# The last chunk of each norm added, squared and summed in two token halves, with fewer identity products around its sums

## The chip, the cores and the metric

The kernel runs on one core of a Trainium2 chip. A core has TensorE (PE, matrix products into PSUM banks; its weight loader is listed apart as PEld), VectorE (DVE), ScalarE (ACT), GpSimd (POOL) and a queue for DMAs (SyncE, SP). They run side by side and wait for one another by semaphores. The metric is the time of one execution on the device in microseconds, lower is better.

## The reference

Two transformer-like blocks on x of 512 tokens by 1024 channels, float32. The first has one layer, modulated by a conditioning vector; the second has two layers. Between their parts stand RMS norms:

```python
def _rmsnorm_2(x, g):
    x32 = x.astype(jnp.float32)
    y = x32 * lax.rsqrt(jnp.mean(x32 * x32, axis=-1, keepdims=True) + RMS_EPS)
    return (y * g.astype(jnp.float32)).astype(x.dtype)

def second_block(x, norm_g, ffn_w_gate, ffn_w_up, ffn_w_down, w_in, conv_w, pool_w, pool_scale, w_out):
    for l in range(DEPTH_2):
        g = norm_g[l]
        f = _swiglu(_rmsnorm_2(x, g[0]), ffn_w_gate[l, 0], ffn_w_up[l, 0], ffn_w_down[l, 0])
        x = x + 0.5 * _rmsnorm_2(f, g[1])
        m = _mixer(_rmsnorm_2(x, g[2]), w_in[l], conv_w[l], pool_w[l], pool_scale[l], w_out[l])
        x = x + _rmsnorm_2(m, g[3])
        f = _swiglu(_rmsnorm_2(x, g[4]), ffn_w_gate[l, 1], ffn_w_up[l, 1], ffn_w_down[l, 1])
        x = x + 0.5 * _rmsnorm_2(f, g[5])
    return x
```

The first block is a mixer (attention and a state-space branch) and a feed-forward part, each behind a modulated norm and added to x through a gate (`gt1`, `gt2`), and a final norm. What matters here is the sum of squares over the 1024 channels, for each token: it needs every channel before any token can be scaled.

## The kernel before

Everything lies with channels on the 128 partitions: x is 8 chunks of 128 channels by 512 tokens (`x[:, c, :]`, `DC` = 8, `T` = 512). A linear layer is a row of *units*; one unit makes one chunk of 128 output channels in one PSUM bank (`unit_bank[s]`, s = 0 or 1 in turn; two units are a *pair* p). Weights and inputs are split into a high and a low part, and each unit multiplies high by high, high by low and low by high (L649 to L651). While TensorE multiplies, SyncE loads later weights, ACT and POOL split them (L1211, L510), and DVE takes finished banks.

Each engine's program is written out by hand in one order; nothing is scheduled later. Waits are `e.wait_ge(semaphore, count)`.

A norm sits between the last unit of one layer and the first of the next. Its work on the eight chunks c = 0 to 7 goes along with the last eight units: DVE takes the bank (`take`, L2211, L2216 or L2220), ACT squares the chunk (`f_squares`: L1228 into `f_sq`, and L1230 into `gf_sq`, scaled by a gain, for the norm that follows), DVE adds the squares to a running sum and, in norms 1 to 5, the products of x and f too (`cross_of`, L2155, and L2158). After chunk 6 the sum of seven chunks is `f_acc`.

The last chunk is what this case is about. TensorE turns squares into sums for each token with `token_sums` (L704): four products with a column of ones, one for each block of 128 tokens, into four columns of a bank. It does so first for `f_acc`, then for the square of the last chunk, `f_sq`, and the two are added up in PSUM. Then ACT takes the root (L1221), DVE the reciprocal (L2193), and `spread` on TensorE (L712) copies the factor of each token to all partitions. DVE updates x chunk by chunk (L2233, L2235), ACT and POOL split the new input, and TensorE starts on it in `first_units` (L725, L735). Between these steps stands `keep_warm(n)` (L699): n products of the identity matrix with itself, whose result nobody reads. A product of float32 values stands in the trace as two records, in the order as one row.

`norm(r)` does this for r = 0 (end of the first block) to 5. The last norm, r = 6, works by token halves already: `last_unit` on TensorE, `last_halves` on DVE (L2104, L2114), and its squares on ACT (L1260). `halves` are the columns 0 to 255 and 256 to 511.

The norm in the middle of the first block (the x1 norm here) is written out apart: DVE's `take_update` (L2021) adds the gated output to x, ACT squares it (`square`, L1217, called from `squares_along`), TensorE sums `x_acc` and then the last square, turns a row of modulation values (`turn_ada`, L925) that ACT has copied (`take_row`, L1326) and spreads the inverse (L1154). ACT takes the root in L1470, DVE the inverse in L2040, and then the gate values (L1791, L1785).

Of the kernel before, what the change touches and what calls it, by code (L numbers as in the profile page):

```python
# [104 lines left out]
def program(nc, d):  # L105
    ctx = ExitStack()
    with ctx:
# [3 lines left out]
        def sem(name):  # L111
            return ctx.enter_context(nc.semaphore(name))
# [190 lines left out]
        pool_step, turn_ready = sem("pool_step"), sem("turn_ready")  # L303
        vec_passed = sem("vec_passed")
        out_stored = sem("out_stored")
        f_scaled, x_summed = sem("f_scaled"), sem("x_summed")

        def col(name, i=0, n=1):
# [326 lines left out]
        def _(e):  # L635
# [60 lines left out]
            def keep_warm(n, bank=mix[1]):  # L696

                for _ in range(n):
                    e.matmul(bank[:, 0:P], tab("ident"), tab("ident"), start=True, stop=True)  # L699

            def token_sums(sums, src, first=True, last=True):

                for b in range(TB):
                    mm = e.matmul(sums[:, b:b + 1], src[:, b * P:(b + 1) * P], tab("ones", 0, 1),  # L704
                                  start=first and b == 0, stop=last and b == TB - 1)
                return mm

            def spread(n, inv, bank):
# [94 lines left out]
            def norm(r):  # L803


                e.wait_ge(fsq_added, (DC - 1) * (r + 1))
                token_sums(square_sum, f_acc, last=False)
                keep_warm(3)
                e.wait_ge(fsq_ready, 2 * DC * r + 2 * (DC - 1) + 1)
                token_sums(square_sum, f_sq, first=False).then_inc(sums_ready, 1)  # L810
                keep_warm(3)
                spread(2 * r + 1, inv_f, stat_bank)

                e.wait_ge(cross_ready, r + 1)
                mm = token_sums(gf_sum, gf_acc)
                if r:
                    mm = token_sums(cross_sum, cross_acc)
                mm.then_inc(cross_sums, 1)
                keep_warm(4)
                first_units(FIRST_OF_NORM + r, 6, lambda: spread(2 * r + 2, inv_u, mix[1]))  # L820
# [322 lines left out]
            sum_rows(score[0])  # L1143
            e.wait_ge(sq_used, DC - 1)
            token_sums(square_sum, x_acc, last=False)
            keep_warm(3)
            e.wait_ge(sq_ready, DC)
            token_sums(square_sum, sq[:, 1, :], first=False).then_inc(x1_sums, 1)
            keep_warm(1)
            turn_ada(2, score[1], TB)  # L1150
            keep_warm(2)
            e.wait_ge(x1_inverse, 1)
            for b in range(TB):
                mm = e.matmul(stat_bank[:, b * P:(b + 1) * P], inv_f[:, b:b + 1].broadcast_to([P, P]), tab("ident"),  # L1154
# [44 lines left out]
        def _(e):  # L1199
# [13 lines left out]
            def square(q, c):  # L1213

                if c >= 2:
                    e.wait_ge(sq_used, DC * q + c - 1)
                e.activation(sq[:, c % 2, :], x[:, c, :], ACT.Square).then_inc(sq_ready, 1)  # L1217
# [5 lines left out]
            def f_squares(p, s, part, c, g):  # L1223

                e.wait_ge(taken[s], p + 2)
                settled()
                fc = part[:, bass.ds(c, 1), :].rearrange("p a t -> p (a t)")
                e.activation(f_sq, fc, ACT.Square).then_inc(fsq_ready, 1)  # L1228
                if g is not None:
                    e.activation(gf_sq, fc, ACT.Square, scale=g(c)).then_inc(fsq_ready, 1)  # L1230

            def first_high(q, s):

                e.wait_ge(first_loaded[s], 16 * (q + 1))
                e.activation(first_hi[:, s, :], first_raw[:, s, :], ACT.Copy).then_inc(first_hi_ready, 1)

            def norm(r, p, part, g):
# [19 lines left out]
                if not ahead:  # L1257
# [16 lines left out]
                            store(n - 1)  # L1274
                    store(len(PE_SUMS) - 1)
                    return
                f_squares(p, 1, part, DC - 1, g)
                e.wait_ge(sums_ready, r + 1)
                token_root(root_f, square_sum)
                for c in range(DC):  # L1280
# [169 lines left out]
            def squares_along(q, p0, refills):  # L1450

                for c in range(DC):
                    if c:
                        e.wait_ge(taken[(c - 1) % 2], p0 + (c - 1) // 2 + 2)
                        square(q, c - 1)
                    if c == refills - 1:
                        for s in range(2):
                            first_high(0, s)
                    if c < refills:
                        refill(p0 + c // 2 + 1, c % 2)  # L1460
                e.wait_ge(taken[1], p0 + DC // 2 + 1)
                square(q, DC - 1)
                take_row(2 * DC + 1, 2, score[0][:])

            e.preload_act_table_set("sqrt_and_others")
# [166 lines left out]
        def _(e):  # L1632
# [10 lines left out]
            def flat(ap):  # L1643
                return ap.rearrange("p a t -> p (a t)")
# [372 lines left out]
            def take_update(p, s, c, gate):  # L2017
# [3 lines left out]
                e.scalar_tensor_tensor(xc, unit_bank[s][:], mod[:, bass.ds(gate + c, 1)], xc, ALU.mult,  # L2021
                                       ALU.add).then_inc(taken[s], 1)

            step(e.memset(stat_bank[:], 0.0))
            for k in range(DC):
                add_ada(k, 64, 2 * DC, ada_shift[k % 3], (*score, *mix), shift_sum)
                if k:
                    e.wait_ge(sq_ready, k)
                    step(e.tensor_tensor(x_acc if k == DC - 1 else stat_bank[:], stat_bank[:], sq[:, (k - 1) % 2, :],
                                         ALU.add))  # L2030
                    e.sem_inc(sq_used, 1)
                take_update(OUT1 + k // 2, k % 2, k, 16)
            def gated_update(p0, gate):
                with e.Fori(0, DC // 2) as i:
                    for s in range(2):
# [98 lines left out]
            def norm(r, p, take, part, g, update):  # L2134
# [25 lines left out]
                def chunk(p, s, c, ahead_of_last=0):  # L2160


                    e.wait_ge(unit_done, 2 * p + s + 1)
                    direct = crossed and take is take_new and ahead_of_last != 1
                    if direct:
                        cross_of(c, unit_bank[s][:])
                    take(p, s, c)
                    if crossed and not direct:
                        e.wait_ge(taken[s], p + 2)
                        cross_of(c, row(f, c))  # L2170
                    if crossed:
                        add_cross(cross_acc if ahead_of_last == 1 else cross_run)
                    if ahead_of_last == 1:
                        return
                    e.wait_ge(fsq_ready, 2 * DC * r + (2 if ahead else 1) * c + 1)
                    step(e.tensor_tensor(f_acc if ahead_of_last == 2 else f_run, f_run, f_sq, ALU.add))
                    if ahead:
                        add_gf(c, gf_run)
                    e.sem_inc(fsq_added, 1)
# [26 lines left out]
                                           ALU.mult, ALU.subtract).then_inc(u_last, 1)  # L2206
                e.wait_ge(rstd_ready, r + 1)

            def take_x(p, s, c):
                xc = flat(x[:, bass.ds(c, 1), :])  # L2210
                e.scalar_tensor_tensor(xc, unit_bank[s][:], mod[:, bass.ds(40 + c, 1)], xc, ALU.mult,  # L2211
                                       ALU.add).then_inc(taken[s], 1)

            def take_f(p, s, c):
                fc = flat(f[:, bass.ds(c, 1), :])
                e.tensor_tensor(fc, unit_bank[s][:], fc, ALU.add).then_inc(taken[s], 1)  # L2216

            def take_new(p, s, c):
                settled()
                e.tensor_copy(flat(f[:, bass.ds(c, 1), :]), unit_bank[s][:]).then_inc(taken[s], 1)  # L2220

            def final_norm(c):
                e.scalar_tensor_tensor(x[:, c, :], x[:, c, :], col("g_final", c), stat_bank[:], ALU.mult,
# [307 lines left out]
```

## Time and profile before

| | us |
|---|---|
| median of 3 runs | 2482.87 |
| lowest, highest | 2482.63, 2484.28 |
| the profiled execution | 2483.62 |
| its span (first to last instruction) | 2481.8 |
| TensorE busy in it | 2468.1 |
| DVE, ACT, POOL busy | 1172.6, 917.1, 1078.8 |

The span is what the trace covers; 1.8 us of the profiled execution lie around it. TensorE's busy time counts the identity products too, so a busy TensorE isn't always a useful one. All times below are microseconds from the start of the span, unless marked ns. The norms' sums of the last chunk stand at 334, 605, 971, 1170, 1537, 1905 and 2103 us of the span.

### The profile page before, as it was taken

To read this page: it belongs to the slowest core of one execution; us is meant where nothing else is said; L and a number is where in the kernel's file an instruction comes from. 1 tells how busy PE (TensorE), PEld (TensorE's weight loads), DVE (VectorE), ACT (ScalarE), POOL (GpSimd) and SP (SyncE) were. 2 spreads that over 40 slices of the span, in tenths; PEclk is the share of its full clock that TensorE was granted. 3 is DMA by queue.
4 is the path that set the end of the run, shared out by engine and by line. 5 is a ranking of instruction groups with operands and counts; after the bars stand their busy time and mean duration, and the time that the engine had idled before them with its cause. 6 is when DMAs were issued, how large, how long until landed. Compare 5 with 4: busy or idle time off the path is not lost.

```text
span 2481.8 us, 33166 instructions
## 1 busy us (share of the span) xinstructions
PE 2468.1 (99%) x11577; PEld 2012.0 (81%) x11577; DVE 1172.6 (47%) x1726; ACT 917.1 (37%) x1307; POOL 1078.8 (43%) x535
## 2 busy tenths in 40 slices
PE   9999999999999999999999999999999999999999
PEld 6777888888888888778888888888888778888887
DVE  7574866264331345676431345331345676431332
ACT  4444443235321334554331234321234454431332
POOL 5333454445344445334444445444445334444444
PEclk9999999999999999999999999999999999999999
DMA  6222643322223221322233232233231322232232
GB/s 253 86 81 92 232 171 118 110 93 77 92 101 105 100 101 62 101 77 93 76 104 107 95 105 72 85 106 106 93 109 61 93 79 100 76 103 86 99 106 81
DMA packets 74059, 253.43 MB, mean 102 GB/s; under 512 B 9184, under 2 KB 13408, under 8 KB 73856
## 3 DMA queue, kind: packets, MB, share of 16 engines
q1 hardware_dynamic: 73408, 251.93, 29.8%
q8 instruction: 44, 0.72, 0.1%
q10 hardware_dynamic: 576, 0.52, 0.1%
q14 instruction: 31, 0.25, 0.0%
HBM read 244.76 MB, written 2.10 MB: 99 GB/s over the span
## 4 chain that ended last, share of the span: by engine, by line
PE 86%; issue 9%; POOL 3%; DVE 2%; ACT 0%; DMA 0%; SPq 0%; POOLq 0%; DVEq 0%; ACTq 0%
PE unit_bank L649 26%; PE unit_bank L650 26%; PE unit_bank L651 26%; POOL w_lo L510 2%; PE score L735 2%; PE score L725 1%; PE mix L868 1%; PE out_bank L848 1%; PE mix L699 1%; PE mix L876 0%; PE out_bank L704 0%; PE score L868 0%; POOL u_lo L609 0%; PE stat_bank L712 0%; DVE arena L1662 0%
## 5 line engine op out<-in xcount | busy, mean ns | idle before, releaser
L510 POOL TENSOR_TENSOR w_lo<-raw,w_hi 128x1024 fp32r<-128x1024 f32 (+2 forms) x374 | 954.2, 2551 | 1301.7 <-ACT w_hi L1211 1301.5
L1211 ACT ACTIVATE w_hi<-raw 128x1024 fp32r<-128x1024 f32 (+2 forms) x375 | 416.1, 1110 | 1203.2 <-PE unit_bank L651 1181.9
L649 PE MATMUL unit_bank<-u_hi,w_hi 128*128 128x512 f32 x2152 | 843.0, 392 | 1.2 <-POOL w_lo L510 1.2
L650 PE MATMUL unit_bank<-u_lo,w_hi 128*128 128x512 f32 x2152 | 837.8, 389 | 0.0
L651 PE MATMUL unit_bank<-u_hi,w_lo 128*128 128x512 f32 x2152 | 837.7, 389 | 0.0
L649 PEld LDWEIGHTS unit_bank<-u_hi,w_hi 128*128 128x128 f32 x2152 | 403.9, 188 | 101.3 <-issue 14.3
L651 PEld LDWEIGHTS unit_bank<-u_hi,w_lo 128*128 128x128 f32 x2152 | 404.0, 188 | 84.6
L650 PEld LDWEIGHTS unit_bank<-u_lo,w_hi 128*128 128x128 f32 x2152 | 404.0, 188 | 82.5 <-issue 0.2
L649 PE MATMUL unit_bank<-h_hi,w_hi 128*128 128x512 f32 x981 | 382.7, 390 | 0.2 <-DVE h_lo L2080 0.2
L651 PE MATMUL unit_bank<-h_hi,w_lo 128*128 128x512 f32 x981 | 381.7, 389 | 0.0
L650 PE MATMUL unit_bank<-h_lo,w_hi 128*128 128x512 f32 x981 | 381.6, 389 | 0.0
L2263 DVE TENSOR_TENSOR arena<-unit_bank,rstd 128x512 f32<-128x512 f32 x84 | 58.1, 691 | 398.9 <-PE unit_bank L651 398.9
L649 PEld LDWEIGHTS unit_bank<-h_hi,w_hi 128*128 128x128 f32 x981 | 184.2, 188 | 39.2 <-DVE h_lo L2080 0.7
L650 PEld LDWEIGHTS unit_bank<-h_lo,w_hi 128*128 128x128 f32 x981 | 184.2, 188 | 38.5 <-issue 0.5
L651 PEld LDWEIGHTS unit_bank<-h_hi,w_lo 128*128 128x128 f32 x981 | 184.1, 188 | 38.4
L2272 DVE TENSOR_TENSOR h_lo<-arena,h_hi 128x512 f32 (+1 forms) x88 | 170.9, 1942 | 78.5 <-ACT h_hi L1535 78.5
L2220 DVE COPY f<-unit_bank 128x512 f32 (+1 forms) x48 | 33.2, 691 | 204.2 <-PE unit_bank L651 202.7
L2260 DVE TENSOR_TENSOR arena<-unit_bank,rstd 128x512 f32<-128x512 f32 x84 | 58.1, 691 | 119.4 <-PE unit_bank L651 119.4
L1535 ACT ACTIVATE h_hi<-arena 128x512 f32 (+1 forms) x88 | 55.6, 632 | 34.0 <-DVE arena L2270 33.4
L2216 DVE TENSOR_TENSOR f<-unit_bank,f 128x512 f32 (+1 forms) x31 | 21.4, 690 | 91.8 <-PE unit_bank L651 90.8
L2270 DVE TENSOR_TENSOR arena<-arena 128x512 f32<-128x512 f32 x88 | 60.9, 693 | 3.3
L609 POOL TENSOR_TENSOR u_lo<-arena,u_hi 128x512 fp32r<-128x512 f32 x42 | 53.2, 1301 | 8.4 <-ACT arena L1477 8.2
(383 smaller groups left out, 2074.4 us busy)
## 6 DMA issues: line engine op xcount, KB each, us to landing
raw<-in_w_gate_up SPq DMA_DIRECT2D x168, 512.0 KB, 3.4
raw<-in_w_down SPq DMA_DIRECT2D x64, 704.0 KB, 4.1
raw<-in_w_in SPq DMA_DIRECT2D x65, 512.0 KB, 3.5
raw<-in_w_up SPq DMA_DIRECT2D x30, 512.0 KB, 3.5
f<-in_w_ada_rows SPq DMA_DIRECT2D x26, 512.0 KB, 5.4
raw<-in_w_out SPq DMA_DIRECT2D x24, 512.0 KB, 3.5
raw<-in_w_down SPq DMA_DIRECT2D x16, 512.0 KB, 3.5
ada_in_u<-in_w_ada SPq DMA_DIRECT2D x8, 512.0 KB, 11.1
```

Source lines behind the costliest of these rows:

```text
L510: e.tensor_tensor(w_lo[:, s, 0:n], raw[:, s, 0:n], as32(w_hi[:, s, 0:n]), ALU.subtract).then_inc(lo_ready, 1)
L609: e.tensor_tensor(u_lo[:, c, :], u_all[:, c, :], as32(u_hi[:, c, :]), ALU.subtract).then_inc(u_ready, 1)
L649: e.matmul(bank[:], wh, hi(k), start=n == 0, stop=False)
L650: e.matmul(bank[:], wh, lo(k), start=False, stop=False)
L651: mm = e.matmul(bank[:], wl, hi(k), start=False, stop=last)
L735: e.matmul(score[s][:], w[:, s, c * P:(c + 1) * P], u_hi[:, c, :], start=c == 0 and w is first_hi, stop=False)
L1211: e.activation(w_hi[:, s, 0:n], raw[:, s, 0:n], ACT.Copy).then_inc(hi_ready, 1)
L1535: e.activation(h_hi[:, bass.ds(i, 1), :].rearrange("p a t -> p (a t)"), ffn_h, ACT.Copy).then_inc(hhi_ready, 1)
L2260: g = e.tensor_tensor(ffn_g, banks[0][:], rstd[:], ALU.mult)
L2263: u = e.tensor_tensor(ffn_u, banks[1][:], rstd[:], ALU.mult)
L2270: e.tensor_tensor(ffn_h, ffn_s, ffn_u, ALU.mult).then_inc(hidden_ready, 1)
L2272: e.tensor_tensor(flat(h_lo[:, bass.ds(i, 1), :]), ffn_h, as32(flat(h_hi[:, bass.ds(i, 1), :])), ALU.subtract).then_inc(h_ready, 1)
```

## The change

The addition of chunk 7 on DVE becomes two operations of 256 tokens each, in the six norms and in the x1 norm. ACT squares each half as soon as it is there, on semaphores of their own (`last_taken` and `taken[1]`, `x_half_taken` and `taken[1]`), and the scaled square into `gf_sq` follows in one piece. TensorE sums blocks 0 and 1 when the first half is squared, blocks 2 and 3 when the second is (`sums_by_halves`). The identity products before and after these sums go from three and three to one and one in the six norms; in the x1 norm those before the sums (three), between the sums and the turn (one) and behind the turn (two) go.

```diff
-            def token_sums(sums, src, first=True, last=True):
-
-                for b in range(TB):
+            def token_sums(sums, src, first=True, last=True, blocks=range(TB)):
+
+                for b in blocks:
                     mm = e.matmul(sums[:, b:b + 1], src[:, b * P:(b + 1) * P], tab("ones", 0, 1),
                                   start=first and b == 0, stop=last and b == TB - 1)
+                return mm
+
+            def sums_by_halves(src, squared, at):
+
+                for hf in range(2):
+                    e.wait_ge(squared, at + hf + 1)
+                    mm = token_sums(square_sum, src, first=False, blocks=(2 * hf, 2 * hf + 1))
                 return mm
...
                 token_sums(square_sum, f_acc, last=False)
-                keep_warm(3)
-                e.wait_ge(fsq_ready, 2 * DC * r + 2 * (DC - 1) + 1)
-                token_sums(square_sum, f_sq, first=False).then_inc(sums_ready, 1)
-                keep_warm(3)
+                keep_warm(1)
+                sums_by_halves(f_sq, last_squared, 2 * r).then_inc(sums_ready, 1)
+                keep_warm(1)
                 spread(2 * r + 1, inv_f, stat_bank)
...
             token_sums(square_sum, x_acc, last=False)
-            keep_warm(3)
-            e.wait_ge(sq_ready, DC)
-            token_sums(square_sum, sq[:, 1, :], first=False).then_inc(x1_sums, 1)
-            keep_warm(1)
+            sums_by_halves(sq[:, 1, :], x_half_squared, 0).then_inc(x1_sums, 1)
             turn_ada(2, score[1], TB)
-            keep_warm(2)
             e.wait_ge(x1_inverse, 1)
...
+            def last_squares(r, p, part, g):
+
+                e.wait_ge(last_taken, r + 1)
+                settled()
+                for hf, cs in enumerate(halves):
+                    if hf:
+                        e.wait_ge(taken[1], p + 2)
+                    e.activation(f_sq[:, cs], part[:, DC - 1, cs], ACT.Square).then_inc(last_squared, 1)
+                e.activation(gf_sq, part[:, DC - 1, :], ACT.Square, scale=g(DC - 1)).then_inc(fsq_ready, 2)
...
-                f_squares(p, 1, part, DC - 1, g)
+                last_squares(r, p, part, g)
...
-                e.wait_ge(taken[1], p0 + DC // 2 + 1)
-                square(q, DC - 1)
+                e.wait_ge(sq_used, DC * q + DC - 2)
+                for hf, cs in enumerate(halves):
+                    if hf:
+                        e.wait_ge(taken[1], p0 + DC // 2 + 1)
+                    else:
+                        e.wait_ge(x_half_taken, 1)
+                    e.activation(sq[:, (DC - 1) % 2, cs], x[:, DC - 1, cs], ACT.Square).then_inc(x_half_squared, 1)
...
+            def last_update(p, gate):
+
+                c = DC - 1
+                e.wait_ge(unit_done, 2 * p + 2)
+                for cs, done in zip(halves, (x_half_taken, taken[1])):
+                    e.scalar_tensor_tensor(x[:, c, cs], unit_bank[1][:, cs], mod[:, gate + c:gate + c + 1], x[:, c, cs],
+                                           ALU.mult, ALU.add).then_inc(done, 1)
...
-                    take(p, s, c)
+                    if ahead_of_last == 1:
+                        for cs, done in zip(halves, (last_taken, taken[s])):
+                            take(p, s, c, cs, done)
+                    else:
+                        take(p, s, c)
...
-            def take_f(p, s, c):
-                fc = flat(f[:, bass.ds(c, 1), :])
-                e.tensor_tensor(fc, unit_bank[s][:], fc, ALU.add).then_inc(taken[s], 1)
+            def take_f(p, s, c, cs=slice(0, T), done=None):
+                fc = flat(f[:, bass.ds(c, 1), cs])
+                e.tensor_tensor(fc, unit_bank[s][:, cs], fc, ALU.add).then_inc(done or taken[s], 1)
```

`take_x` and `take_new` get the same two arguments. `ahead_of_last == 1` marks the last chunk.

TensorE in norm 1, from the sums of `f_acc` (first row) to the spread of the inverse. `arena` holds the squares and their sums, `tabs` the identity and the ones, `mix1` is the bank that the identity products write. Before:

```order
L704 MATMUL out_bank<-tabs,arena 128x1 [waits fsq_added]
L704 MATMUL out_bank<-tabs,arena 128x1 x3
L699 MATMUL mix1<-tabs 128x128 x3
L704 MATMUL out_bank<-tabs,arena 128x1 [waits fsq_ready]
L704 MATMUL out_bank<-tabs,arena 128x1 x3
L699 MATMUL mix1<-tabs 128x128 x3
L712 MATMUL stat_bank<-tabs,arena 128x128 [waits inverse_ready]
```

The same stretch of TensorE in the changed kernel:

```order
L706 MATMUL out_bank<-tabs,arena 128x1 [waits fsq_added]
L706 MATMUL out_bank<-tabs,arena 128x1 x3
L701 MATMUL mix1<-tabs 128x128
L706 MATMUL out_bank<-tabs,arena 128x1 [waits last_squared]
L706 MATMUL out_bank<-tabs,arena 128x1
L706 MATMUL out_bank<-tabs,arena 128x1 [waits last_squared]
L706 MATMUL out_bank<-tabs,arena 128x1
L701 MATMUL mix1<-tabs 128x128
L721 MATMUL stat_bank<-tabs,arena 128x128 [waits inverse_ready]
```

The wait for the square has become two, one for each half, and four of six identity products are gone.

TensorE in the x1 norm, from the sums of `x_acc` to the spread (L1154, later L1158), with the turn of the modulation row (L925, later L933) between. Before:

```order
L704 MATMUL out_bank<-tabs,arena 128x1 [waits sq_used]
L704 MATMUL out_bank<-tabs,arena 128x1 x3
L699 MATMUL mix1<-tabs 128x128 x3
L704 MATMUL out_bank<-tabs,arena 128x1 [waits sq_ready]
L704 MATMUL out_bank<-tabs,arena 128x1 x3
L699 MATMUL mix1<-tabs 128x128
L925 MATMUL score1<-tabs,arena 128x128 [waits row_ready]
L925 MATMUL score1<-tabs,arena 128x128 x3
L699 MATMUL mix1<-tabs 128x128 x2
L1154 MATMUL stat_bank<-tabs,arena 128x128 [waits x1_inverse]
```

The same stretch of TensorE in the changed kernel:

```order
L706 MATMUL out_bank<-tabs,arena 128x1 [waits sq_used]
L706 MATMUL out_bank<-tabs,arena 128x1 x3
L706 MATMUL out_bank<-tabs,arena 128x1 [waits x_half_squared]
L706 MATMUL out_bank<-tabs,arena 128x1
L706 MATMUL out_bank<-tabs,arena 128x1 [waits x_half_squared]
L706 MATMUL out_bank<-tabs,arena 128x1
L933 MATMUL score1<-tabs,arena 128x128 [waits row_ready]
L933 MATMUL score1<-tabs,arena 128x128 x3
L1158 MATMUL stat_bank<-tabs,arena 128x128 [waits x1_inverse]
```

No identity product is left between the first sums and the spread.

DVE in norm 1, from the addition of the last chunk to the reciprocal and the scaled sum behind it. Before:

```order
L2216 TENSOR_TENSOR f<-unit_bank1,f 128x512 [waits vec_step,unit_done]
L2155 SCALAR_TENSOR_TENSOR arena<-x,half_g,f 128x512 [waits consts_loaded,cols_loaded,taken1]
L2158 TENSOR_TENSOR arena<-mix0,arena 128x512 [waits vec_step]
L2193 RECIPROCAL arena<-arena 128x4 [waits root_ready,vec_step]
L2151 TENSOR_TENSOR arena<-score1,arena 128x512 [waits fsq_ready]
```

The same stretch of DVE in the changed kernel:

```order
L2249 TENSOR_TENSOR f<-unit_bank1,f 128x256 [waits vec_step,unit_done]
L2249 TENSOR_TENSOR f<-unit_bank1,f 128x256
L2184 SCALAR_TENSOR_TENSOR arena<-x,half_g,f 128x512 [waits consts_loaded,cols_loaded,taken1]
L2187 TENSOR_TENSOR arena<-mix0,arena 128x512 [waits vec_step]
L2226 RECIPROCAL arena<-arena 128x4 [waits root_ready,vec_step]
L2180 TENSOR_TENSOR arena<-score1,arena 128x512 [waits fsq_ready]
```

The addition is split; the cross product behind it still waits for all of the chunk, and the reciprocal for the cross sum.

## Rows read from the trace of the kernel before

**Rows 1.** The page's first two parts: TensorE's busy time and granted clock

```profile
PE 2468.1 (99%) x11577; PEld 2012.0 (81%) x11577; DVE 1172.6 (47%) x1726; ACT 917.1 (37%) x1307; POOL 1078.8 (43%) x535
...
PEclk9999999999999999999999999999999999999999
```

**Rows 2.** Chain of waits in norm 1: start us, us, what

```profile
970.64 0.78 PE mix L699 x6
971.42 0.94 PE out_bank L704 x8
972.36 0.78 PE mix L699 x6
```

**Rows 3.** Timeline of norm 1: start us, us, engine line op, [idle before <-releaser]

```profile
969.89 0.69 DVE L2216 TENSOR_TENSOR f<-unit_bank,f 128x512 f32<-128x512 f32 x1 [3.80 <-PE unit_bank L651]
970.48 0.75 PEld L699 LDWEIGHTS mix<-tabs 128*128 128x128 f32 x6
...
970.62 0.63 ACT L1228 ACTIVATE arena<-f 128x512 f32<-128x512 f32 x1 [6.01 <-DVE f L2216]
970.62 0.75 DVE L2155 SCALAR_TENSOR_TENSOR arena<-x,half_g,f 128x512 f32<-128x512 f32 x1
971.16 0.71 ACT L1230 ACTIVATE arena<-f,half_g 128x512 f32<-128x512 f32 x1
971.30 0.97 PEld L704 LDWEIGHTS out_bank<-tabs,arena 128*128 128x128 f32 x8
...
971.41 0.69 DVE L2158 TENSOR_TENSOR arena<-mix,arena 128x512 f32<-128x512 f32 x1
972.19 0.75 PEld L699 LDWEIGHTS mix<-tabs 128*128 128x128 f32 x6
...
972.40 0.26 ACT L1221 ACTIVATE arena<-out_bank,eps 128x4 f32<-128x4 f32 x1 [0.53 <-PE out_bank L704]
972.76 0.18 DVE L2193 RECIPROCAL arena<-arena 128x4 f32<-128x4 f32 x1 [0.66 <-ACT arena L1221]
...
972.99 0.97 PEld L712 LDWEIGHTS stat_bank<-tabs,arena 128*128 128x128 f32 x8
```

**Rows 4.** The line L2193: number, duration ns min/median/max, first and last start

```profile
L2193 DVE RECIPROCAL arena<-arena x6: 177/178/179, 606.2 to 2104.8; 128x4 f32<-128x4 f32 x6
```

**Rows 5.** Timeline of the last norm, operations on halves of the tokens

```profile
2466.23 0.42 DVE L2104 TENSOR_TENSOR f<-unit_bank,f 128x256 f32<-128x256 f32 x1 [1.87 <-PE unit_bank L759]
...
2466.69 0.42 ACT L1260 ACTIVATE arena<-f 128x256 f32<-128x256 f32 x1 [3.05 <-DVE f L2104]
...
2470.44 0.87 DVE L2114 SCALAR_TENSOR_TENSOR f<-f,half_g,stat_bank 128x256 f32<-128x256 f32 x2 [1.90 <-PE stat_bank L783]
```

**Rows 6.** Timeline of the x1 norm

```profile
331.91 0.75 DVE L2021 SCALAR_TENSOR_TENSOR x<-unit_bank,mod,x 128x512 f32<-128x512 f32 x1 [1.46 <-PE unit_bank L651]
...
333.68 0.75 PEld L699 LDWEIGHTS mix<-tabs 128*128 128x128 f32 x6
...
334.35 0.97 PEld L704 LDWEIGHTS out_bank<-tabs,arena 128*128 128x128 f32 x8
...
335.45 0.26 ACT L1470 ACTIVATE arena<-out_bank,eps 128x4 f32<-128x4 f32 x1 [1.64 <-PE out_bank L704]
335.47 0.47 PEld L925 LDWEIGHTS score<-tabs,arena 128*128 128x128 f32 x4
...
335.75 0.18 DVE L2040 RECIPROCAL arena<-arena 128x4 f32<-128x4 f32 x1 [3.08 <-ACT arena L1470]
...
336.35 0.97 PEld L1154 LDWEIGHTS stat_bank<-tabs,arena 128*128 128x128 f32 x8
336.42 0.17 DVE L1785 SCALAR_TENSOR_TENSOR amp<-mod,cols 128x8 f32<-128x8 f32 x1
```

**Rows 7.** Windows: us, busy PE PEld DVE ACT POOL (x), granted clock, DMA

```profile
16.00:20.00 4.00, 3.25 (x35) 2.15 (x32) 3.73 (x10) 0.26 (x1) 3.32 (x9) 1.00 1.05 392
...
976.60:989.08 12.48, 12.26 (x59) 9.64 (x58) 10.06 (x16) 11.07 (x17) 10.35 (x12) 1.00 0.01 2
```

More of the change, by code:

```diff
@@ L305, in program @@
         out_stored = sem("out_stored")
+        last_taken, last_squared = sem("last_taken"), sem("last_squared")
+        x_half_taken, x_half_squared = sem("x_half_taken"), sem("x_half_squared")
         f_scaled, x_summed = sem("f_scaled"), sem("x_summed")
@@ L2031, in _ @@
                     e.sem_inc(sq_used, 1)
-                take_update(OUT1 + k // 2, k % 2, k, 16)
+                if k < DC - 1:
+                    take_update(OUT1 + k // 2, k % 2, k, 16)
+            last_update(OUT1 + DC // 2 - 1, 16)
             def gated_update(p0, gate):
@@ L2207, in norm, with take_x, take_new @@
                 e.wait_ge(rstd_ready, r + 1)
[L2209 to L2212, printed above, removed]
-            def take_f(p, s, c):
-                fc = flat(f[:, bass.ds(c, 1), :])
-                e.tensor_tensor(fc, unit_bank[s][:], fc, ALU.add).then_inc(taken[s], 1)
-            def take_new(p, s, c):
+            def take_x(p, s, c, cs=slice(0, T), done=None):
+                xc = flat(x[:, bass.ds(c, 1), cs])
+                e.scalar_tensor_tensor(xc, unit_bank[s][:, cs], mod[:, bass.ds(40 + c, 1)], xc, ALU.mult,
+                                       ALU.add).then_inc(done or taken[s], 1)
+            def take_f(p, s, c, cs=slice(0, T), done=None):
+                fc = flat(f[:, bass.ds(c, 1), cs])
+                e.tensor_tensor(fc, unit_bank[s][:, cs], fc, ALU.add).then_inc(done or taken[s], 1)
+            def take_new(p, s, c, cs=slice(0, T), done=None):
                 settled()
-                e.tensor_copy(flat(f[:, bass.ds(c, 1), :]), unit_bank[s][:]).then_inc(taken[s], 1)
+                e.tensor_copy(flat(f[:, bass.ds(c, 1), cs]), unit_bank[s][:, cs]).then_inc(done or taken[s], 1)
             def final_norm(c):
```

## The prediction

> **What bounds the kernel now.** I read the page first. TensorE is busy for 99% of the span and its granted clock is full in every slice [rows 1], so a change can gain only where TensorE's own list of instructions gets shorter, or where that list waits for a result that now comes sooner. The change touches seven places: the norm after the first block's mixer, which I call the x1 norm, and the six norms that `norm(r)` computes. At each of them TensorE stops multiplying weights and a short loop of engines runs instead: DVE adds the last chunk, ACT squares it, TensorE sums it, ACT takes the root, DVE inverts it, TensorE spreads it over the rows.
>
> I next read the chain of waits of one such norm [rows 2]. It seems to say that TensorE is the bound all through: sums, six records of the identity products (`keep_warm`, L699), sums, six records more, then the spread. Two records are one product. Taken at its word, every product that is dropped would give back 0.78 / 3 = 0.26 us. The chain goes back along an engine as long as that engine never stood still, and the identity products are there so that it doesn't; so the order in time has to be read beside it.
>
> That order [rows 3] shows two loops that end together. The last chunk is added on DVE (969.89 + 0.69 = 970.58), squared on ACT (970.62 + 0.63 = 971.25), and its sums start at 971.30. The first three identity products leave the weight loader at 970.48 + 0.75 = 971.23. So the sums wait for the square and for the products alike: neither alone gives back more than 0.07 us. Behind the sums the root (972.40 + 0.26 = 972.66) and the inverse (972.76 + 0.18 = 972.94) end, and the spread starts at 972.99. The second three products run from 972.19 to 972.94, exactly as long. They too lie beside a wait that would be there without them. The reciprocal stands six times in the trace with the same length [rows 4], and the six norms repeat this pattern; norm 0 lacks only the cross products (L2155, L2158).
>
> **The six norms, part by part.** The added chunk is now taken in two operations of 256 columns, and the square is too. Such halves stand in the last norm, which worked this way before [rows 5]: an addition out of PSUM takes 0.42 us, two operations in a row 0.87 us for two, which is a step of about 0.41, and a square 0.42. The first square starts 0.46 us after the start of its addition (2466.23 to 2466.69).
>
> On norm 1's clock: first half added 969.89 to 970.31, squared 970.35 to 970.77; second half added up to 970.71, squared 970.75 to 971.17. TensorE needs 0.05 us from a square's end to the first load of its sums (971.25 to 971.30) [rows 3]. It has left the earlier sums at 970.48 and the one product that stays at 970.48 + 0.25 = 970.73, so it starts the first two blocks at 970.82, not at 971.30. Eight records take 0.89 us to the next instruction (971.30 to 972.19), so half of them end at 971.27, and the second square has been there for TensorE since 971.22. The sums go through without a new wait, 0.48 us earlier, with a margin of only 0.05.
>
> What is late next? On ACT, the scaled square (L1230, 0.71 long, 0.54 behind a square) is queued ahead of the root. It now starts behind the second half, at about 971.1, and ends at 971.8; the root is wanted at 971.92. That cover holds, by 0.1 us. On DVE, the cross product waits for both halves, so it starts at 970.75 and not at 970.62; with the add behind it (0.79 later, 0.69 long) it ends at 972.23, and the reciprocal waits for that too. The root would let it start at 972.76 - 0.48 = 972.28. These two ends now nearly coincide, and for a few hundredths that this may cost I take 0.45 us for each norm in place of 0.48. The second group of products shrinks from three to one; with that TensorE stands idle for about half a microsecond before the spread, which costs nothing, since it waited for the reciprocal anyway. Everything behind the spread is paced by it: first update on DVE, first products, u_lo on POOL. So the shift is kept. Six norms: 6 x 0.45 = 2.7 us.
>
> Bounds for one norm: were the square no hindrance, TensorE could start at 970.73, which gives 971.30 - 970.73 = 0.57. From below, the halves could hand over worse than the last norm's do: each of two handovers 0.1 later leaves 0.28, and I set 0.25. Six norms: 1.5 to 3.4.
>
> A rule of the Trainium skill speaks against the change: "VectorE: DVE Perf Modes", section "The TRN2 errata", says that an operation on VectorE and ScalarE pays a fixed latency each time, and advises tiles of at least 512 elements. Here the rows agree as to the fixed part: 0.42 for half against 0.69 for the whole on DVE [rows 3, 5], so 0.15 us are paid twice, and on ACT 0.21. By the rule alone, with the two engines one behind the other, a norm would lose 2 x 0.42 + 2 x 0.42 - 0.69 - 0.63 = 0.36 us. It doesn't weigh that the first half's square runs beside the second half's addition.
>
> **The x1 norm** [rows 6]. Here TensorE itself is what is late. The update is added at 331.91; by halves, each 0.45 long, the second one is added by about 332.75 and squared by 333.25, before the sums of x_acc have left TensorE at 333.68. So the new sums follow at once, at 333.68 in place of 334.35: 0.67 us. The root goes from 335.45 to 334.78, the reciprocal from 335.75 to 335.08, ending at 335.26. Of the other three products one stood before the turn of the modulation row (L925) and two behind it. Without them the turn (0.47) ends on the weight loader at about 335.05, and the spread waits for the reciprocal instead and starts at 335.26 + 0.05 = 335.31, not at 336.35: 1.04 us. The gate values (L1785) ended at 336.59, 0.93 before the spread was through, and move up with the turn. Bounds: 0.67, if the products behind the turn hid something that I don't see, to 336.35 - 335.1 = 1.25, if the reciprocal comes sooner than counted.
>
> **Sum.** 2.7 + 1.04 = 3.7 us. The profiled execution took 2483.62 us (span 2481.8): 2479.9 after. The median of the three runs, 2482.87, is 0.75 below the profiled one; on that scale I forecast 2479.1. The forecast's own range is 2482.87 - 3.4 - 1.25 = 2478.2 to 2482.87 - 1.5 - 0.67 = 2480.7. A measurement of this kernel can tell about 0.2%, 5.0 us, from no change; the forecast lies within it, on the fast side.
>
> **Rivals.**
> 1. *The chain at its word.* Thirty products go: 4 x 6 in the norms, 6 in the x1 norm. At 0.26 us each that is 7.8 us: 2475.1. For it: TensorE is never idle there [rows 2]. Against: the two loops beside the products, which end at the same hundredth [rows 3]. Chance 0.07.
> 2. *The halves don't pay in the six norms.* The second half's square misses the 0.05 us of margin, or the cross product holds the reciprocal, by as much as was won; only the x1 norm gains. 2482.87 - 1.04 = 2481.8. For it: the thin margins and the fixed cost paid twice. Against: the last norm hands over its halves as I counted [rows 5]. Chance 0.13.
> 3. *Slower: TensorE's clock falls.* The products kept TensorE at work. If the gap before the spread, of about 0.5 us, together with the short operations around it lets the clock drop from 2.4 to 1.2 GHz, the first units of that norm run at half pace. They fill 12.48 us at the full level [rows 7], so one norm would lose up to 12.5 us: 2482.87 - 3.7 + 12.5 = 2491.6. It outweighs the gain from 3.7 us of TensorE work at the lower level, and is over 0.2% slower from 8.7 us. Against: between 16 and 20 us TensorE was busy for 3.25 of 4.00 us and the granted clock stayed 1.00 [rows 7]; the new gap is smaller. The Trainium skill, "TensorE: Matmul & The Clock Gate", section "A second HAM failure mode: psum-queue depth-cycling", reports a kernel whose clock went up and down through short idle spells between groups of matmuls; no row here shows that. Chance 0.05.
>
> The remaining chance, 0.75, is the forecast's. Of it and of what I haven't thought of I put 0.08 above a gain of 0.2%, since a repeated measurement can lie off by a microsecond and the x1 norm's upper bound adds to it. So: faster by over 0.2%: 0.07 + 0.08 = 0.15. Slower: 0.05. Within: 0.80. The range for 8 in 10 reaches from 2477.8 to 2482.0; it takes in rival 2 and leaves out rivals 1 and 3.
>
> **What would show it.** In the profile after, for norm 1: the sums of the squares start about 0.5 us after the second addition's start, in one row of eight records without idle time between its halves; root, reciprocal and spread each about 0.45 earlier against the last weight product; TensorE idle for about 0.5 us before the spread, released by the reciprocal. In the x1 norm the spread starts 3.4 us behind the addition and not 4.44. The stages between the norms keep their lengths, and the granted clock stays 1.00. The forecast is wrong if TensorE shows idle time between the two halves of the sums, if the reciprocal is released by DVE's own add well after the root, or if a norm's first units get longer.

## The result: slower, by 0.34%

| | us |
|---|---|
| before, median of 7 runs (lowest, highest) | 2482.87 (2482.63, 2484.38) |
| changed, median of 7 runs (lowest, highest) | 2491.72 (2488.36, 2494.56) |
| ratio, 95% interval | 1.0034 [1.0025, 1.0043] |
| profiled execution of the changed kernel | 2489.88 (span 2487.7) |

I had forecast 2479.1, within 2477.8 to 2482.0, and given a slower kernel a chance of 0.05. The changed kernel loses 8.9 us, and its executions lie 6 us apart where those before lay 1.8 apart.

### The profile after

The page's row of the granted clock still shows a 9 in all 40 slices. A slice is 62 us long and a 9 stands for 90% or more, so a drop of some microseconds can't be seen there. The mean over the whole core shows it:

```profile
core 0: 2487.7 us, clock 0.994
```

The seven executions have mean clocks of 0.995 (2488.36 us) to 0.992 (2494.56 us): the slower an execution, the lower its clock.

The timeline of norm 1 in the changed kernel, to be laid beside [rows 3] (the lines have moved: L2216 is now L2249, L1228 is L1243, L704 is L706, L699 is L701, L1221 is L1225, L2193 is L2226, L712 is L721):

```profile
967.61 0.76 DVE L2249 TENSOR_TENSOR f<-unit_bank,f 128x256 f32<-128x256 f32 x2 [3.81 <-PE unit_bank L653]
968.07 0.75 ACT L1243 ACTIVATE arena<-f 128x256 f32<-128x256 f32 x2 [5.74 <-DVE f L2249]
...
968.54 0.97 PEld L706 LDWEIGHTS out_bank<-tabs,arena 128*128 128x128 f32 x8
...
969.43 0.30 PEld L701 LDWEIGHTS mix<-tabs 128*128 128x128 f32 x2
...
969.63 0.27 ACT L1225 ACTIVATE arena<-out_bank,eps 128x4 f32<-128x4 f32 x1 [0.20 <-PE out_bank L706]
970.00 0.18 DVE L2226 RECIPROCAL arena<-arena 128x4 f32<-128x4 f32 x1
...
970.23 1.26 PEld L721 LDWEIGHTS stat_bank<-tabs,arena 128*128 128x128 f32 x8 [0.50 <-DVE arena L2226]
970.23 1.55 PE L721 MATMUL stat_bank<-tabs,arena 128*128 128x128 f32 x8 [0.31 <-DVE arena L2226]
971.37 3.53 PEld L706 LDWEIGHTS mix<-tabs,arena 128*128 128x128 f32 x16
```

Up to the spread, everything is as I had worked it out. From the start of the addition to the first load of the sums it takes 968.54 - 967.61 = 0.93 us, before 1.41; to the spread 2.62, before 3.10. The eight records of the sums run through in 0.97 us, without a gap between the halves. But then TensorE's weight loader (PEld) stands idle for 0.50 us and its matrix part (PE) for 0.31. During the spread the pace breaks: its eight loads take 1.26 us, before 0.97, and the sixteen behind it 3.53. In the kernel before those sixteen took 1.86 (from 973.88).

Windows of the changed kernel: norm 0, then norm 1 in three pieces. Columns as in [rows 7]; the one after POOL is the granted clock.

```profile
601.36:619.25 17.89, 17.61 (x101) 14.96 (x100) 9.16 (x15) 13.21 (x23) 10.67 (x9) 1.00 0.07 27
967.41:970.70 3.29, 2.98 (x25) 2.74 (x24) 2.90 (x6) 1.63 (x4) 0.00 (x0) 1.00 0.00 0
970.70:977.50 6.80, 6.80 (x33) 6.66 (x32) 5.59 (x10) 3.20 (x6) 1.91 (x6) 0.51 0.00 0
977.50:988.98 11.48, 11.48 (x55) 9.59 (x54) 7.69 (x11) 8.55 (x14) 9.31 (x7) 0.99 0.01 2
```

For 6.8 us the clock was at 1.2 GHz (0.51 of full), and then it was back. That happens in norms 1, 2, 3 and 5, and for half as long in norm 4; not in norm 0, where the matrix part idles for 0.24 us before the spread. To see what it costs I take the length of a norm from its first sums to the next layer's first unit out of `unit_bank` (in norm 1 before: 969.70 to 989.30). Norms 0 to 5 in the order of time:

| | norm 0 | 1 | 2 | 3 | 4 | 5 |
|---|---|---|---|---|---|---|
| before | 18.37 | 19.60 | 19.62 | 19.62 | 19.61 | 19.63 |
| changed | 17.89 | 21.57 | 21.53 | 21.56 | 19.93 | 21.56 |

Norm 0 gains 0.48. The others lose 1.9 each, norm 4 0.3. The x1 norm, from its first sums, takes 16.67 instead of 17.74. Together that is -1.07 - 0.48 + 1.97 + 1.91 + 1.94 + 0.32 + 1.93 = +6.5 us. The two profiled spans differ by 5.9; the x1 norm begins 0.7 us earlier in this one (332.07 against 332.80), a part of the program that the change doesn't touch. So the norms account for the difference.

TensorE's waits in the changed kernel have one row that the kernel before didn't have (in all, times, longest):

```profile
PE stat_bank L721 <- DVE arena L2226: 1.8, 6, 0.3
```

### The profile page after: what moved, and what is told of

It reads as the page before. It is cut to its first block, busy times and chain, and to the rows that moved or that the text cites. A ratio compares the mean times of both kernels' runs of the same rounds, so it can differ in the third digit from the quotient of the medians.

```text
span 2487.7 us, 33062 instructions
## 1 busy us (share of the span) xinstructions
PE 2474.1 (99%) x11517; PEld 2019.4 (81%) x11517; DVE 1175.0 (47%) x1733; ACT 917.1 (37%) x1314; POOL 1079.7 (43%) x535
## 4 chain that ended last, share of the span: by engine, by line
PE 87%; issue 9%; POOL 2%; DVE 1%; ACT 0%; DMA 0%; SPq 0%; POOLq 0%; DVEq 0%; ACTq 0%
PE unit_bank L651 26%; PE unit_bank L652 26%; PE unit_bank L653 26%; PE score L744 2%; POOL w_lo L512 2%; PE score L734 1%; PE mix L876 1%; PE out_bank L856 1%; PE mix L701 1%; PE mix L706 1%; PE mix L884 0%; PE out_bank L706 0%; PE stat_bank L721 0%; PE score L876 0%; DVE arena L1681 0%
## 5 line engine op out<-in xcount | busy, mean ns | idle before, releaser
L2253 DVE COPY f<-unit_bank 128x512 f32 (+2 forms) x50 | 33.3, 670 | 204.6 <-PE unit_bank L653 203.1
L2249 DVE TENSOR_TENSOR f<-unit_bank,f 128x512 f32 (+2 forms) x34 | 21.6, 642 | 91.8 <-PE unit_bank L653 90.8
```

## The experiments

Theories: **A**, the clock falls because TensorE now stands idle for a few tenths of a microsecond in a stretch of short products (the *gap* below). **B**, what counts is the number of identity products around the sums. **C**, the split itself does it. All runs are compared with the kernel before on the same chip (medians 2483.05, 2482.83 and 2483.10 on the three chips). The falls are counted in one profiled execution of each kernel; the mean clock is known for every execution.

### Three products behind the sums

```diff
                 keep_warm(1)
                 sums_by_halves(f_sq, last_squared, 2 * r).then_inc(sums_ready, 1)
-                keep_warm(1)
+                keep_warm(3)
```

> The changed kernel with one number put back: three identity products behind the sums of the squares in the six norms, not one. Halves and everything else as changed. Theory A (the clock falls because TensorE stands idle between the sums and the spread): the idle time of 0.3 to 0.5 us before the spread is filled again, the granted clock stays 1.00, and the gain of the shorter chain is left: about 2479.2 us, 3.7 below the kernel before. Theory B (what counts is how many identity products run around the sums in all, wherever they stand): four of six are back, the clock falls in some of the norms, 2482 to 2488. Theory C (the split itself, with its extra wait on TensorE, brings the clock down): it stays near 2491.

Measured: 2479.71 (10 runs, 2479.38 to 2480.74), ratio 0.9986 [0.9976, 0.9996]. Norm 1's timeline in this kernel:

```profile
968.56 0.97 PEld L706 LDWEIGHTS out_bank<-tabs,arena 128*128 128x128 f32 x8
...
969.45 0.75 PEld L701 LDWEIGHTS mix<-tabs 128*128 128x128 f32 x6
...
970.25 0.97 PEld L721 LDWEIGHTS stat_bank<-tabs,arena 128*128 128x128 f32 x8
971.13 1.86 PEld L706 LDWEIGHTS mix<-tabs,arena 128*128 128x128 f32 x16
```

The sums and the spread stand where they stand in the changed kernel, to 0.02 us; two products fill the gap between them, and the sixteen loads are back at 1.86. The norms take 17.86 and 19.12 to 19.17. A as forecast: the products that looked free to drop were the ones that paid.

### Three ahead of the sums, one behind

```diff
-                keep_warm(1)
+                keep_warm(3)
                 sums_by_halves(f_sq, last_squared, 2 * r).then_inc(sums_ready, 1)
                 keep_warm(1)
```

> The changed kernel with three identity products ahead of the sums of the squares in the six norms, and one behind. Theory A (idle time before the spread): that idle time stays, so the clock still falls; the sums are held back by 0.4 us too: 2490 to 2494. Theory B (their number in all): as many products as with three behind, so the same few falls, 2482 to 2488, or none, about 2482.

Measured: 2489.55 (10 runs, 2483.21 to 2497.57), ratio 1.0021 [1.0009, 1.0032], just under the range expected. As many products in all as in the run above, and the clock falls in all of norms 1 to 5 of the profiled execution (19.12 to 19.17 was their length with three behind; here 20.26 to 23.48). B is out: the place decides. In this profile the clock fell in the x1 norm too, which is the same code in the changed kernel:

```profile
332.29:342.29 10.00, 9.93 (x60) 9.01 (x57) 4.41 (x9) 6.47 (x13) 3.81 (x4) 0.83 0.50 204
```

That cost 17.40 - 16.67 = 0.73 us there.

### One and one, without halves

```diff
-                keep_warm(3)
+                keep_warm(1)
                 e.wait_ge(fsq_ready, 2 * DC * r + 2 * (DC - 1) + 1)
                 token_sums(square_sum, f_sq, first=False).then_inc(sums_ready, 1)
-                keep_warm(3)
+                keep_warm(1)
```

(against the kernel before)

> The kernel before with one identity product on each side of the sums in the six norms, no halves, and the middle norm of the first block as before. Theories A and B: TensorE idles ahead of the sums (0.5 us, for the square) and behind them, the clock falls as in the changed kernel or more often, and nothing is won: 2492 to 2496. Theory C (the split itself): the clock stays 1.00 and the time is that of before, 2482.9, or some tenths less.

Measured: 2500.96 (4 runs, 2499.31 to 2503.60), ratio 1.0069 [1.0052, 1.0086]: worse than expected, and worse than the changed kernel. The clock falls in all six norms, norm 0 too (22.43 us). C is out.

### The split alone

```diff
-                keep_warm(1)
+                keep_warm(3)
                 sums_by_halves(f_sq, last_squared, 2 * r).then_inc(sums_ready, 1)
-                keep_warm(1)
+                keep_warm(3)
...
+            keep_warm(3)
             sums_by_halves(sq[:, 1, :], x_half_squared, 0).then_inc(x1_sums, 1)
+            keep_warm(1)
             turn_ada(2, score[1], TB)
+            keep_warm(2)
```

> The changed kernel with all identity products of before put back, in the six norms and in the middle norm of the first block: the split alone. Theories A and B: the clock stays 1.00, and the split gains nearly nothing, since the products ahead of the sums hold them as before: 2482.4 to 2482.9. Theory C: the clock falls in norms 1 to 5 as in the changed kernel, 2490 or more.

Measured: 2482.54 (10 runs, 2482.12 to 2484.11), ratio 0.9998 [0.9988, 1.0007]. The norms take 18.15 and 19.46 to 19.48, so the split alone gives 0.14 to 0.22 us each. In the six norms this kernel differs from the one with three behind only in the products ahead of the sums, three and not one, and that one is 0.3 us a norm shorter: those products held the rest, as read from [rows 3]. It takes the halves and the fewer products ahead of the sums to get some 0.47; the products dropped behind the sums add nothing. Its profiled execution, the slowest of its ten, had a fall of the clock in the start-up:

```profile
16.00:20.00 4.00, 2.67 (x29) 1.66 (x28) 3.73 (x11) 0.26 (x1) 3.30 (x9) 1.00 1.04 386
20.00:24.00 4.00, 4.00 (x28) 2.29 (x26) 2.35 (x15) 0.00 (x0) 2.00 (x9) 0.57 1.05 408
```

This is the stretch that I had used as evidence that idle time is harmless [rows 7]. But it isn't equally idle in all profiles: 0.75 us of 4.00 in the kernel before and 0.95 without halves, both without a fall behind it, and 1.33 here.

### How much idle time, and of what

Two products behind the sums:

```diff
                 sums_by_halves(f_sq, last_squared, 2 * r).then_inc(sums_ready, 1)
-                keep_warm(1)
+                keep_warm(2)
```

> The changed kernel with two identity products behind the sums of the squares in the six norms, not one and not three. Theory A (idle time of TensorE before the spread): about half of the idle time is left. If any idle time does it, the clock still falls in some norms, 2482 to 2489; if its length counts, the clock stays 1.00 and the time is that of three products, 2479.7. Theory B (the number of products in all) has been left by the run with three ahead of the sums.

Measured: 2483.70 (10 runs, 2479.48 to 2492.66), ratio 1.0009 [0.9999, 1.0018]. The ten values come in steps: 2479.48 once (mean clock 1.000); 2483.50 to 2483.85 six times (0.998); 2487.28 and 2487.76 (0.996); 2492.66 (0.993). In the profiled one, a 2483.7, norm 1 alone had a fall and took 23.20 us, 4.07 more than the other norms of this kernel (19.12 to 19.14). So a step of 4 us fits one fall; that the executions at 0.996 had two is inferred, since only one execution is profiled.

By its own terms the expectation's first case came true (any idle time does it). But there are fewer falls than in the changed kernel, so the length of the gap counts too.

The same with one product of 128 columns and one of 256:

```diff
                 sums_by_halves(f_sq, last_squared, 2 * r).then_inc(sums_ready, 1)
                 keep_warm(1)
+                e.matmul(mix[1][:, 0:2 * P], tab("ident"), tabs[:, 0:2 * P], start=True, stop=True)
```

> The changed kernel, and behind the sums of the squares in the six norms one identity product of 128 columns and one of 256 columns: two products, that keep TensorE at work about as long as three small ones. Theory A (TensorE's time at work before the spread is what counts): no idle time before the spread, clock 1.00, about 2479.7 as with three. Rival D (the number of products behind the sums counts): as with two products, a fall in most executions, 2483.5.

Measured: 2480.01 (10 runs, 2479.27 to 2482.65), ratio 0.9988 [0.9978, 0.9998]. No fall in the profile. Two products, one wider, do what three small ones did, but for one run at 2482.65. Five of the ten executions have a mean clock of 0.999, as four of ten had with three behind. The rows tell what differs. The first 3.30 us of norm 2, from its first sums to about the spread, with two products behind:

```profile
1169.52:1172.82 3.30, 3.22 (x27) 2.98 (x26) 2.92 (x6) 1.62 (x4) 0.00 (x0) 1.00 0.34 129
```

and with one small and one wide:

```profile
1165.56:1168.86 3.30, 3.30 (x27) 2.98 (x26) 2.92 (x6) 1.63 (x4) 0.00 (x0) 1.00 0.34 137
```

The weight loader idles alike in both (2.98 of 3.30 busy); the matrix part idles for 0.08 us in the one and not at all in the other. So the loader's idle time doesn't bring the clock down in this profile, and the matrix part's may. Two limits: the profile models the ends of products, so 0.08 us is a small figure for it; and the wide product fills the gap and is more work too, which this run doesn't separate.

### Where the idle time may lie

Two products more, but behind the spread:

```diff
                 mm.then_inc(cross_sums, 1)
-                keep_warm(4)
+                keep_warm(6)
```

> The changed kernel with six identity products, not four, between the sums for the next norm and the first units: the two that were dropped behind the sums are run again, but 2 us later, where TensorE doesn't wait. Theory A: the idle time before the spread is as in the changed kernel, so the clock falls in most of norms 1 to 5, and the two products may hold the first unit back by up to 0.4 us in each norm: 2490 to 2494. Rival (what counts is the work around the spread as a whole, wherever the idle time lies): the clock stays 1.00 in most norms, 2479.7 plus at most 2.4, so 2480 to 2482.

Measured: 2492.71 (9 runs, 2488.82 to 2495.72), ratio 1.0036 [1.0026, 1.0046]. The clock falls in all six norms. Work that comes later doesn't make up for the gap.

None ahead of the sums, three behind, so that the gap lies ahead of the sums:

```diff
-                keep_warm(1)
                 sums_by_halves(f_sq, last_squared, 2 * r).then_inc(sums_ready, 1)
-                keep_warm(1)
+                keep_warm(3)
```

> The changed kernel with no identity product ahead of the sums of the squares in the six norms and three behind. TensorE then idles for about 0.3 us ahead of the sums, where it waits for the first half's square, and not before the spread. If only idle time right before the spread does it (because the spread and what follows are short products too), the clock stays 1.00 and the time is 2479.7. If idle time of this length anywhere between the last weight product and the first unit does it (theory A in its wide form), the clock falls in most executions, 2483 to 2492.

Measured: 2490.94 (10 runs, 2483.43 to 2496.39), ratio 1.0031 [1.0018, 1.0043]. It is A in its wide form: idle time ahead of the sums does it too. In the profile norms 3 to 5 fell (23.03 to 23.19 us), norms 1 and 2 did not (19.15), with the same idle time in all five. Whether one gap brings the clock down thus varies from norm to norm, and nothing in these rows says why.

The first 3.30 us of norm 2 in three kernels, the one before, the changed one and this one:

```profile
1167.95:1171.25 3.30, 3.30 (x30) 3.17 (x28) 2.37 (x5) 1.51 (x3) 0.00 (x0) 1.00 0.38 150
```

```profile
1167.62:1170.92 3.30, 3.00 (x25) 2.76 (x24) 2.92 (x6) 1.63 (x4) 0.00 (x0) 1.00 0.36 139
```

```profile
1165.00:1168.30 3.30, 3.12 (x27) 2.98 (x26) 2.92 (x6) 1.63 (x4) 0.00 (x0) 1.00 0.37 144
```

With the same row of the other kernels, the last two below included (the idle time is that of norms 1 to 5, where it varies by 0.01 within a kernel, but for norm 5 without halves, 0.33), the runs line up:

| kernel | idle in it, us | norms with a fall, of 6 | median |
|---|---|---|---|
| before; split alone; three behind; one small and one wide; first block's norm alone; best version | 0.00 | 0 | 2482.9; 2482.5; 2479.7; 2480.0; 2482.3; 2479.6 |
| two behind | 0.08 | 1 | 2483.7 |
| none ahead, three behind | 0.18 | 3 | 2490.9 |
| changed | 0.30 | 5 | 2491.7 |
| two more behind the spread | 0.30 | 6 | 2492.7 |
| three ahead | 0.31 | 5 | 2489.6 |
| one and one, without halves | 0.63 | 6 | 2501.0 |

Norm 0 has a gap of its own: 0.24 us with one product behind or none ahead. There the clock fell in one profile of four (two more behind the spread), though the 0.18 us of norms 3 to 5 above were enough. So the length of the gap isn't all; where it lies counts too.

### The first block's norm alone, and the best version

```diff
             token_sums(square_sum, x_acc, last=False)
-            keep_warm(3)
-            e.wait_ge(sq_ready, DC)
-            token_sums(square_sum, sq[:, 1, :], first=False).then_inc(x1_sums, 1)
-            keep_warm(1)
+            sums_by_halves(sq[:, 1, :], x_half_squared, 0).then_inc(x1_sums, 1)
             turn_ada(2, score[1], TB)
-            keep_warm(2)
```

(against the kernel before, with the halves of its update and square)

> Of the change only the norm in the middle of the first block: its last update by halves and its six identity products dropped; the six other norms as before. By my sum it is worth 1.0 us (1.07 by the trace of the changed kernel): 2482.0 against 2483.05, with the clock at 1.00. If the dropped products bring the clock down there too in some executions, the median stays near 2482 and single runs lie 1 to 3 us above.

Measured: 2482.29 (11 runs, 2481.70 to 2484.08), ratio 0.9998 [0.9989, 1.0007]: the median is 0.54 lower, where 1.0 was expected, and the time doesn't separate it from no change. Its trace shows the norm at 16.67 us against 17.74. Of the eight runs with a mean clock of 1.000 seven lie at 2481.70 to 2482.46 and one at 2483.09; the other three, at 0.999, at 2483.24 to 2484.08. Here too the weight loader idles for 0.31 us before the spread. I took that for TensorE's idle time; the matrix part idles for 0.07 only. The first 3.30 us of this norm in the changed kernel:

```profile
332.07:335.37 3.30, 3.23 (x31) 2.99 (x28) 0.52 (x3) 1.19 (x4) 0.00 (x0) 1.00 1.03 415
```

Eight of the profiled kernels have this gap, and the clock fell behind it in one, that with three ahead. The last version puts one product into it, and three behind the sums in the norms:

```diff
             turn_ada(2, score[1], TB)
+            keep_warm(1)
             e.wait_ge(x1_inverse, 1)
```

> The version that the runs so far point to: the changed kernel with three identity products behind the sums in the six norms, and one behind the turn of the modulation row in the middle norm of the first block, where TensorE idled for 0.31 us before the spread. Theory A: no fall of the clock anywhere, 2479.3 to 2479.7, with less spread among its runs than with three behind alone (2479.38 to 2480.74).

Measured: 2479.60 (11 runs, 2479.31 to 2480.30) against 2482.83, ratio 0.9987 [0.9978, 0.9996], faster than both kernels. All eleven runs have a mean clock of 1.000, where four of ten with three behind alone had 0.999. With one small and one wide, where this gap is open too, it was five of ten. That fits a fall in the gap now and then, but which place fell in those executions isn't known. The medians of the two (2479.60 and 2479.71) don't differ, and this run still spreads over 1 us, so what the one product is worth isn't settled.

## Why the prediction was wrong

**The step that failed** is the sentence "with that TensorE stands idle for about half a microsecond before the spread, which costs nothing, since it waited for the reciprocal anyway". I priced the products dropped there by what they delay, which is nothing, and not by what they do. The idle time was right (in norm 1 0.50 on the loader, 0.31 on the matrix part); its price was 8.9 + 3.3 = 12 us for the kernel, the distance between the changed kernel and the same with the two products back.

**Rival 3 was the right mechanism, with too small a chance.** I held against it one stretch of one execution, 3.25 of 4.00 us busy and the clock at 1.00. The runs show the fall to vary from norm to norm and from execution to execution, and in another profile, where that stretch idled for 1.33 us and not 0.75, it happened right behind it. One row of a clock that stayed up, from another place in the program, is weak evidence. Its size was off both ways: a fall costs 0.7 to 4.1 us and not up to 12.5, because the clock comes back within 3 to 10 us (6.8 in norm 1) and part of that time TensorE waits anyway. In norm 1, 6.8 us at half pace do the work of 3.4, and the norm got 21.57 - 19.12 = 2.4 longer than with three behind: there it takes 3.6 us from the start of the first pair of `score` products to that of the seventh, and 2.7 for the next six, so 0.9 us of waiting was there to be used up. But a fall comes in up to six norms of an execution, where I priced one. That my figure for this rival, 2491.6, is the measured median is luck: two errors that cancel.

**The chain's gain was right.** The six norms: forecast 0.45 each, measured 0.48 in norm 0 of the changed kernel and 0.45 to 0.49 in norms 1 to 5 once the clock holds (with three behind; 19.60 to 19.12 in norm 1). The x1 norm: forecast 1.04, measured 1.07; its spread starts 3.40 us behind the addition, as forecast:

```profile
331.18 0.88 DVE L2048 SCALAR_TENSOR_TENSOR x<-unit_bank,mod,x 128x256 f32<-128x256 f32 x2 [1.46 <-PE unit_bank L653]
...
334.58 0.97 PEld L1158 LDWEIGHTS stat_bank<-tabs,arena 128*128 128x128 f32 x8 [0.31 <-DVE arena L2069]
```

The sum of these lengths is 3.9 us; the medians of the best version and of three behind show 3.2 and 3.3. Most of the rest lies outside the span. The median span is 3.6 and 3.75 us shorter than before (2477.4 against 2481.0, 2477.55 against 2481.3), but 2.2 us of an execution lie around the span and no longer 1.8. That is so in all kernels with halves in the six norms; those without them have 1.8 or 1.9. No run shows what these 0.4 us are, and I had carried the 1.8 over. The last 0.15 to 0.3 us are less than the start of the x1 norm moves from profile to profile (331.95 to 333.79).

**Rival 1**, the chain at its word, would have been 7.8 us. The three products that the chain counts behind the sums (0.78 us) are cover: with one there the spread stands at 970.23, with three at 970.25. **Rival 2**, that the halves don't pay, is refuted by three behind: the second half met the first without a gap. The advice of the Trainium skill that the prediction weighed ("VectorE: DVE Perf Modes", "The TRN2 errata": tiles of at least 512 elements) didn't decide. The trace agrees that halves cost more in themselves, two of them 0.76 us on DVE against 0.69 and 0.75 on ACT against 0.63, but the two engines overlapped, and the sums started 0.48 us sooner.

## What to carry to other kernels

Products whose result nobody reads may be what keeps TensorE's clock up; before dropping one, ask whether TensorE idles in its place, and price that by what runs next at half pace, not by what it delays. Drop such products only where they make TensorE late for its next operand, and leave in, or add, as many as fill the wait that is left. Read the granted clock from windows of a few microseconds, and from several executions: an average over slices, or one profile without a fall, doesn't show that it is safe.

## What the runs showed of the hardware

These are counts from one profiled execution of each kernel, with idle times of the matrix part as the profile models them. In norms 1 to 5, within a stretch of short products that was otherwise busy, a gap of 0.08 us was followed by a fall to 1.2 GHz in one of five norms, 0.18 in three, and 0.30 or more in all five, in four kernels; without a gap there was no fall in six kernels. A second count supports the smallest figure: with the 0.08 us, nine of ten executions had a mean clock of 0.998 or less, and with three products behind none of ten.

Idle time of the weight loader alone (0.32 of 3.30 us) was not followed by a fall in the profile. A gap ahead of the sums did it as one behind them did. But the gap's length doesn't decide alone: 0.24 us in norm 0 were followed by a fall in one profile of four, 0.07 in the x1 norm in one of eight, and in the start-up (16 to 20 us) up to 0.95 us of 4.00 in none and 1.33 in the one profile that had it. Whether a short gap among the long products of a layer would do it was not tried.

The falls in norms 1 to 5 lasted 3.4 to 10.2 us. The shortest made its norm 0.8 us longer (19.93 us), those of 6.8 us 2.4 (21.57) and the longest about 4.0 (23.20).
